# x loaded first, set 0 of the first modulation split in two, and three modulation sets moved into the first loop

## The chip, the cores and the metric

One core of a Trainium2 chip runs the whole block in one launch. The metric is device time in microseconds, the median of three runs.

## What is computed

One layer of a streaming encoder on a sequence of 256 frames of width 2048, in float32. The conditioning vector c gives, through one large matrix, nine vectors of 2048: shift, scale and gate for each of three sublayers.

```python
c_act = silu(c)
mod = c_act @ w_ada + b_ada                      # w_ada 2048 x 18432
sh1, sc1, g1, sh2, sc2, g2, sh3, sc3, g3 = split(mod, 9)
hn = rms(h, norm_ffn1) * (1 + sc1) + sh1
h = h + 0.5 * g1 * (silu(hn @ w1) * (hn @ w3)) @ w2      # first FFN, D_FF 5632
hn = rms(h, norm_mix) * (1 + sc2) + sh2
h = h + g2 * mixer(hn)                           # SSD mixer and sparse attention
hn = rms(h, norm_ffn2) * (1 + sc3) + sh3
h = h + 0.5 * g3 * (silu(hn @ w1b) * (hn @ w3b)) @ w2b   # second FFN
```

## The kernel before

All weights are read once. They come in **units** of 128 x 1024 floats (512 KB), 850 in all. A unit's way: SP loads it into one of four `raw` slots (`load_unit`, L610); ScalarE (ACT) rounds it into `w_hi` (`cast`, L807); VectorE (DVE) forms `w_lo = raw - w_hi` (`sub`, L1246, called the split); TensorE (PE) does twelve matmuls, hi times hi, lo times hi, hi times lo (`unit`, L1948 to L1950). A load waits for the split three units back, a cast for PE's unit four back; every engine works through its own list in order.

`w_ada` comes in **pieces** of 512 KB as well, 128 rows by 1024 columns. VectorE multiplies a piece by its entry of silu(c) and adds it to `ada_acc` (L1356 for the first 64 pieces, L1263 and L1266 for the others): 16 pieces to 1024 columns of the modulation. The first 64 pieces hold shift and scale of the first FFN. They form four sets (`SET_TILES`), each of four column tiles of x; piece m of a set is row block m. Their ring has eight slots (`ada_raw`, `ada_more`). A few pieces (`ADA_SHARE`) are taken by PE (`share`, L1990) instead of VectorE. When a set's pieces are in, PE sums `ada_acc` over partitions with `ones` (`sum_first`, L2029), VectorE adds the bias (`mod_first`, L1302, L1306), ACT modulates the set's tiles of x (`rows_of_set`, L897, L901), and VectorE forms their low part (`lo`, L1396). A unit of w1 or w3 with index u needs tile pair u of x.

The later columns (`ada_add`) have a ring of four; after 16 pieces VectorE folds `ada_acc` (`fold`, L1281, L1284: four transposes and four reductions into `fold_s`), and PE sums the folds at the end of the FFN (`sum_folds`).

The first FFN has an **early** stage of 112 units in an order written out by hand (`EARLY`), so that PE has work on tile pairs that are ready, and then a loop `Fori` of three bodies of 48 units. In the early stage `SUM_AT` says before which unit PE makes a set's sum, `KEPT`, `KEPT_TO` and `ADDED` how partial products are put aside and added again, `UNIT_LOADS` after which piece SP loads a unit, `UNIT_SPLITS` after which piece VectorE splits it. `turn_act` transposes the hidden block, `y_add` (L1461) adds w2 products to y. Pieces 16 to 63 stand between units 3 and 44. Three more sets (`ADA_PEELED`) stand beside units 45 to 104, one piece after 4 of 5 units, and one set in each loop body, one piece after every second unit. The mixer and the second FFN take the rest.

At the start x is loaded behind two pieces; ACT squares it (`square`), VectorE adds the sums (`sum_squares`, L1335), POOL forms rstd (L727), ACT scales x into y (L854), PE transposes y (`turn_x`), ACT stages it (`stage`, L840).

Of the kernel before, what the change touches and what calls it, by code (L numbers as in the profile page):

```python
# [60 lines left out]
ADA_MIX = ADA_FIRST + ADA_PEELED[0] + TRIPS[0]  # L61
# [51 lines left out]
def build(nc, x, c, positions, w_ada, b_ada, norm_ffn1, ffn1_w1, ffn1_w3, ffn1_w2, norm_mix, w_in,  # L113
# [288 lines left out]
    SET_TILES = ((0, 4), (4, 4), (8, 4), (12, 4))  # L402
    SET_START = (0, 16, 32, 48, 64)
# [10 lines left out]
    EARLY = (some("w3", 1, (0, 1)) + some("w1", 0, (0,)) + some("w1", 2, (0, 1)) + some("w1", 0, (1,))  # L414
             + some("w3", 2, (0, 1)) + some("w3", 0, (0,)) + some("w1", 3, (0, 1)) + some("w3", 0, (1,))
# [23 lines left out]
    UNIT_SPLITS = (16, 17, 18, 19) + tuple(19 + (u - 3) * 8 // 7 for u in range(4, LATE[0] - 2))  # L439
# [134 lines left out]
    def ada_unit_after(where, w):  # L574
# [3 lines left out]
        elif where == "trip":  # L578
            at = [6 + 2 * i for i in range(KT)]
# [25 lines left out]
    def _(sp):  # L605
# [634 lines left out]
    def _(dve):  # L1240
# [165 lines left out]
        def norm_first():  # L1406

            turned = [j for j in range(UPB)]
            for m in range(PIECES):
# [11 lines left out]
                if e and at >= 2 and turned and SET_ORDER[turned[0]] < e:  # L1421
# [58 lines left out]
        def early_step(n):  # L1480
# [17 lines left out]
            ada_peeled(0)  # L1498

        def ffn(f):  # L1500
# [25 lines left out]
            def hidden(n, o, adds, w0=0, ada=None, after_second=False):  # L1526


                for u in range(BLOCK):
                    if n.per:  # L1530
                        sub(n + u)
                        k = ada_unit_after("trip", w0 + u)
                        if ada and k is not None:
                            ada_add(At(ada.n0 * KT + k, KT, ada.trip), k)
# [19 lines left out]
            with dve.Fori(0, TRIPS[f]) as trip:  # L1554
                piece = At(ADA_FIRST + ADA_PEELED[0], 1, trip)
# [378 lines left out]
    def _(pe):  # L1934
# [18 lines left out]
        def sum_folds(i, bank):  # L1953
# [4 lines left out]
            pe.wait_ge(fold_step, 2 * (ADA_COLS // FOLD_COLS) * (last - ADA_FIRST))  # L1958
# [570 lines left out]
```

## Time and profile before

| | |
|---|---|
| median of three runs | 2612.09 us (2611.2 to 2614.87) |
| the profiled execution | 2613.14 us |
| its span in the trace | 2611.4 us |
| PE, DVE, ACT busy | 98%, 71%, 44% |
| mean granted clock of PE | 0.989 |
| DMA | 609.98 MB, mean 234 GB/s |

The span runs from the first to the last instruction; 1.7 us lie around it. PE's busy time counts pipelined matmuls to their modelled ends, so a busy PE isn't PE at its peak; how many units a stretch did tells more.

### The profile page before, as it was taken

To read this page: it belongs to the slowest core of one execution; us is meant where nothing else is said; L and a number is where in the kernel's file an instruction comes from. 1 tells how busy PE (TensorE), PEld (TensorE's weight loads), DVE (VectorE), ACT (ScalarE), POOL (GpSimd) and SP (SyncE) were. 2 spreads that over 40 slices of the span, in tenths; PEclk is the share of its full clock that TensorE was granted. 3 is DMA by queue.
4 is the path that set the end of the run, shared out by engine and by line. 5 is a ranking of instruction groups with operands and counts; after the bars stand their busy time and mean duration, and the time that the engine had idled before them with its cause. 6 is when DMAs were issued, how large, how long until landed. Compare 5 with 4: busy or idle time off the path is not lost.

```text
span 2611.4 us, 34332 instructions
## 1 busy us (share of the span) xinstructions
PE 2546.2 (98%) x12494; PEld 2146.7 (82%) x12494; DVE 1852.6 (71%) x2032; ACT 1151.2 (44%) x1365; POOL 68.4 (3%) x72
## 2 busy tenths in 40 slices
PE   6999999999998999999999999999999999999998
PEld 5877888888887999898788888887788888888886
DVE  5779987676766888876876677776679655555555
ACT  4434444444444555544456444443544444444442
POOL 1000000000002000000000000000300000000000
PEclk9989999999999999999999999999999999999999
DMA  9988978787865777744454687787499666666664
GB/s 333 341 308 305 332 274 288 225 284 223 280 225 193 256 263 266 254 145 130 129 169 129 209 289 255 254 285 240 138 317 334 193 193 188 190 192 189 190 192 145
DMA packets 288177, 609.98 MB, mean 234 GB/s; under 512 B 23426, under 2 KB 24004, under 8 KB 287172
## 3 DMA queue, kind: packets, MB, share of 16 engines
q1 hardware_dynamic: 285840, 600.78, 70.0%
q10 hardware_dynamic: 1700, 4.58, 0.5%
q0 software_dynamic: 528, 3.17, 0.3%
q8 instruction: 68, 1.11, 0.2%
q14 instruction: 41, 0.34, 0.0%
HBM read 604.24 MB, written 4.22 MB: 233 GB/s over the span
## 4 chain that ended last, share of the span: by engine, by line
PE 81%; DVE 10%; DMA 5%; issue 3%; ACT 1%; POOL 0%; SPq 0%; DVEq 0%; ACTq 0%; POOLq 0%
PE psum L1948 23%; PE psum L1950 22%; PE psum L1949 22%; PE psum L2227 3%; PE psum L2228 3%; PE psum L2229 3%; PE psum L2250 2%; DVE w_lo L1246 2%; DMA ada_raw<-in_w_ada 2%; PE psum L1936 2%; DMA ada_more<-in_w_ada 1%; DVE ada_acc L1266 1%; DVE ada_acc L1356 1%; DVE y L1461 1%; DMA gate_ffn<-gate_rows 1%
## 5 line engine op out<-in xcount | busy, mean ns | idle before, releaser
L1246 DVE TENSOR_TENSOR w_lo<-raw,w_hi 128x1024 fp32r<-128x1024 f32 x850 | 1034.0, 1221 | 538.8 <-ACT w_hi L807 537.9
L807 ACT ACTIVATE w_hi<-raw 128x1024 fp32r<-128x1024 f32 x850 | 897.2, 1060 | 1010.7 <-PE psum L1950 881.9
L1948 PE MATMUL psum<-w_hi,xT_hi 128*128 128x512 f32 x1984 | 789.3, 398 | 6.9 <-issue 5.2
L1949 PE MATMUL psum<-w_lo,xT_hi 128*128 128x512 f32 x1984 | 777.5, 392 | 0.0
L1950 PE MATMUL psum<-w_hi,xT_lo 128*128 128x512 f32 x1984 | 777.3, 392 | 0.0
L1948 PEld LDWEIGHTS psum<-w_hi,xT_hi 128*128 128x128 f32 x1984 | 375.6, 189 | 89.7 <-issue 11.9
L1950 PEld LDWEIGHTS psum<-w_hi,xT_lo 128*128 128x128 f32 x1984 | 375.2, 189 | 79.3
L1949 PEld LDWEIGHTS psum<-w_lo,xT_hi 128*128 128x128 f32 x1984 | 375.7, 189 | 76.0
L1948 PE MATMUL psum<-w_hi,aT_hi 128*128 128x512 f32 x704 | 277.9, 395 | 7.8 <-DVE aT_lo L1449 4.0
L1950 PE MATMUL psum<-w_hi,aT_lo 128*128 128x512 f32 x704 | 276.3, 392 | 0.0
L1949 PE MATMUL psum<-w_lo,aT_hi 128*128 128x512 f32 x704 | 276.2, 392 | 0.0
L1266 DVE SCALAR_TENSOR_TENSOR ada_acc<-ada_raw,cact,ada_acc 128x1024 f32<-128x1024 f32 x210 | 269.3, 1282 | 0.1
L2227 PE MATMUL psum<-xT_hi,w_hi 128*128 128x256 f32 x640 | 183.6, 287 | 4.9 <-DVE xT_lo L1401 4.3
L2228 PE MATMUL psum<-xT_lo,w_hi 128*128 128x256 f32 x640 | 182.0, 284 | 0.0
L2229 PE MATMUL psum<-xT_hi,w_lo 128*128 128x256 f32 x640 | 182.0, 284 | 0.0
L1948 PEld LDWEIGHTS psum<-w_hi,aT_hi 128*128 128x128 f32 x704 | 133.6, 190 | 37.8 <-DVE aT_lo L1449 4.4
L1950 PEld LDWEIGHTS psum<-w_hi,aT_lo 128*128 128x128 f32 x704 | 133.6, 190 | 28.1
L1949 PEld LDWEIGHTS psum<-w_lo,aT_hi 128*128 128x128 f32 x704 | 133.8, 190 | 27.6
L1461 DVE TENSOR_TENSOR y<-psum,y 128x1024 f32<-128x1024 f32 x101 | 123.3, 1221 | 40.4 <-PE psum L1950 40.4
L2227 PEld LDWEIGHTS psum<-xT_hi,w_hi 128*128 128x128 f32 x640 | 123.3, 193 | 6.0 <-DVE xT_lo L1401 4.9
L2228 PEld LDWEIGHTS psum<-xT_lo,w_hi 128*128 128x128 f32 x640 | 123.5, 193 | 0.0
L2229 PEld LDWEIGHTS psum<-xT_hi,w_lo 128*128 128x128 f32 x640 | 123.4, 193 | 0.0
(252 smaller groups left out, 1937.0 us busy)
## 6 DMA issues: line engine op xcount, KB each, us to landing
raw<-in_ffn_w SPq DMA_DIRECT2D x528, 512.0 KB, 4.5
ada_raw<-in_w_ada SPq DMA_DIRECT2D x256, 512.0 KB, 6.0
raw<-in_w_in SPq DMA_DIRECT2D x224, 512.0 KB, 3.8
ada_more<-in_w_ada SPq DMA_DIRECT2D x32, 512.0 KB, 7.0
raw<-in_w_br_ssd SPq DMA_DIRECT2D x32, 512.0 KB, 5.4
raw<-in_w_br_att SPq DMA_DIRECT2D x32, 512.0 KB, 4.8
raw<-in_w_out SPq DMA_DIRECT2D x32, 512.0 KB, 5.1
h<-in_x SPq DMA_DIRECT2D x1, 2048.0 KB, 9.8
```

Source lines behind the costliest of these rows:

```text
L807: nc.scalar.activation(w_hi[:, n.slot(SPLIT), 0:size], raw[:, n.slot(RAW), 0:size], ACT.Copy).then_inc(hi_ready, 1)
L1246: nc.vector.tensor_tensor(w_lo[:, n.slot(SPLIT), 0:size], raw[:, n.slot(RAW), 0:size], w_hi[:, n.slot(SPLIT), 0:size], ALU.subtract).then_ ...
L1266: nc.vector.scalar_tensor_tensor(out=acc[:], in0=src, scalar=cact[:, k:k + 1], in1=acc[:], op0=ALU.mult, op1=ALU.add).then_inc(ada_used, 1)
L1461: nc.vector.tensor_tensor(y[:, :, cols], psum[:, bank:bank + HALF, :], y[:, :, cols], ALU.add).then_inc(y_added, 1)
L1936: return nc.tensor.transpose(dst, src, ident[0:rows_, 0:rows_])
L1948: nc.tensor.matmul(o, hi[:, kt + k, toks], whi, start=a, stop=False)
L1949: nc.tensor.matmul(o, hi[:, kt + k, toks], wlo, start=False, stop=False)
L1950: ins = nc.tensor.matmul(o, lo[:, kt + k, toks], whi, start=False, stop=b)
L2227: nc.tensor.matmul(o, w_hi[:, s, cols], xT_hi[:, kt + k, :], start=a, stop=False, skip_group_check=True)
L2228: nc.tensor.matmul(o, w_hi[:, s, cols], xT_lo[:, kt + k, :], start=False, stop=False, skip_group_check=True)
L2229: ins = nc.tensor.matmul(o, w_lo[:, s, cols], xT_hi[:, kt + k, :], start=False, stop=b, skip_group_check=True)
L2250: return nc.tensor.matmul(o, a, b, start=first, stop=last)
```

## The change

- SP loads x before any piece.
- The first set of 16 pieces is two of eight: `SET_TILES` has five sets, the first two of two tiles each, and each of their pieces holds two row blocks of 512 columns in two DMAs. The order of the first twelve early units, the points of the sums, loads and splits follow; PE makes the sum of set 0 between the transposes of x, the sum of set 1 before unit 2, of set 2 before unit 13, of sets 3 and 4 before units 26 and 40, as sets 2 and 3 before.
- `ADA_SHARE` keeps its first three pieces; VectorE takes the other three.
- `ADA_PEELED[0]` is 0 and `ADA_TRIP` 2: the early stage has no later pieces, a loop body has 32, three after four units up to unit 42, and two folds. Before, a body had 16, so of the six sets in the loop three are new there.
- The small loads and the exponential of a_exp on ACT stand later; `rows_of_set` follows a cast earlier (n - 2 for n - 3).

```diff
-ADA_SHARE = (1, 6, 11, 30, 46, 62)
+ADA_SHARE = (1, 6, 11)
-ADA_PEELED = (3, 2)
+ADA_PEELED = (0, 2)
+ADA_TRIP = 2
...
-    SET_TILES = ((0, 4), (4, 4), (8, 4), (12, 4))
-    SET_START = (0, 16, 32, 48, 64)
+    SET_TILES = ((0, 2), (2, 2), (4, 4), (8, 4), (12, 4))
+    SET_START = (0, 8, 16, 32, 48, 64)
...
-    EARLY = (some("w3", 1, (0, 1)) + some("w1", 0, (0,)) + some("w1", 2, (0, 1)) + some("w1", 0, (1,))
-             + some("w3", 2, (0, 1)) + some("w3", 0, (0,)) + some("w1", 3, (0, 1)) + some("w3", 0, (1,))
+    EARLY = (some("w1", 0, (0,)) + some("w3", 0, (0,)) + some("w3", 1, (0, 1)) + some("w1", 2, (0, 1))
+             + some("w1", 0, (1,)) + some("w3", 2, (0, 1)) + some("w3", 0, (1,)) + some("w1", 3, (0, 1))
...
-    SUM_AT = {at_unit["w1", 1, 0]: 1, at_unit["w1", 1, 2]: 2, at_unit["w1", 1, 4]: 3}
+    SUM_AT = {at_unit["w3", 1, 0]: 1, at_unit["w1", 1, 1]: 2, at_unit["w1", 1, 2]: 3, at_unit["w1", 1, 4]: 4}
...
-    UNIT_LOADS = (13, 15, 16, 17) + tuple(17 + (u - 3) * 8 // 7 for u in range(4, LATE[0]))
+    UNIT_LOADS = ((3, 5, 8, 11, 14) + tuple(16 + (u - 5) * 4 // 3 for u in range(5, 17))
+                  + tuple(32 + (u - 17) * 8 // 7 for u in range(17, LATE[0])))
...
         elif where == "trip":
-            at = [6 + 2 * i for i in range(KT)]
+            at = [1 + i * 4 // 3 for i in range(ADA_TRIP * KT)]
...
+        sp.dma_start(h[:], x[0].rearrange("(s p) d -> p s d", p=P)).then_inc(x_in, 16)
         for m in range(PIECES):
             load_first(m)
-            if m == 1:
-                sp.dma_start(h[:], x[0].rearrange("(s p) d -> p s d", p=P)).then_inc(x_in, 16)
...
+            cast_units(1)
             act.wait_ge(rstd_ready, 1)
...
-            for j in range(UPB):
+            for j in range(4):
+                stage(0, j)
+            cast_units(2)
+            rows_of_set(0)
+            for j in range(4, UPB):
                 stage(0, j)
             cast_units(SPLIT)
...
-            rows_of_set(0)
-            small_loads()
...
-                if n - 3 in SUM_AT:
-                    rows_of_set(SUM_AT[n - 3])
-                    if SUM_AT[n - 3] == 1:
-                        a_exp_out()
+                if n - 2 in SUM_AT:
+                    rows_of_set(SUM_AT[n - 2])
+                if n == at_unit["w2", 0, 0]:
+                    small_loads()
+                if n == at_unit["w2", 3, 0]:
+                    a_exp_out()
...
+                if m == 2:
+                    sum_squares(0)
...
-                if m == 9:
-                    sum_squares(0)
-                if e and at == 1:
+                if e and at == 0:
                     mod_first(e - 1)
...
-                            ada_add(At(ada.n0 * KT + k, KT, ada.trip), k)
+                            ada_add(At(ada.n0 * KT + k, ada.per * KT, ada.trip), k % KT)
+                            if k % KT == KT - 1:
+                                fold(ada + k // KT)
...
-        share(ADA_SHARE[2])
         warm_up(2)
...
-        sum_first(0)
+            if j == 3:
+                sum_first(0)
         warm_up(3)
+        share(ADA_SHARE[2])
```

PE before its first unit; the y rows are transposes of x, L1990 is a piece taken by PE, L2029 (L2042 after) a sum. Before:

```order
L1990 MATMUL psum<-cact,ada_raw 128x1 x8
L1998 MATMUL psum<-h,ident 128x512 x2
L1936 MATMUL psum<-ident,y 128x128 x32
L2029 MATMUL psum<-ones,ada_acc_103 128x1 x8
L1998 MATMUL psum<-h,ident 128x512 x3
```

After:

```order
L2011 MATMUL psum<-h,ident 128x512 x2
L1946 MATMUL psum<-ident,y 128x128 x16
L2042 MATMUL psum<-ones,ada_acc_103 128x1 x8
L1946 MATMUL psum<-ident,y 128x128 x16
L2011 MATMUL psum<-h,ident 128x512 x3
L2003 MATMUL psum<-cact,ada_raw 128x1 x8
```

The sum of set 0 has moved ahead of half of the transposes, and PE's third piece behind all of them.

VectorE in the loop body, units 5 to 9 (w_lo is a split). Before:

```order
L1246 TENSOR_TENSOR w_lo<-raw,w_hi 128x1024
L1244 REGISTER_ALU
L1246 TENSOR_TENSOR w_lo<-raw,w_hi 128x1024
L1258 ISA
L1263 TENSOR_SCALAR ada_acc_103<-ada_raw,cact 128x1024
L1244 REGISTER_ALU
L1246 TENSOR_TENSOR w_lo<-raw,w_hi 128x1024
L1449 TENSOR_TENSOR aT_lo<-psum,aT_hi 128x1024
L1244 REGISTER_ALU
L1246 TENSOR_TENSOR w_lo<-raw,w_hi 128x1024
L1265 ISA
L1266 SCALAR_TENSOR_TENSOR ada_acc_103<-ada_raw,cact,ada_acc_103 128x1024
```

After:

```order
L1257 TENSOR_TENSOR w_lo<-raw,w_hi 128x1024
L1269 ISA
L1276 REGISTER_ALU
L1277 SCALAR_TENSOR_TENSOR ada_acc_103<-ada_raw,cact,ada_acc_103 128x1024
L1255 REGISTER_ALU
L1257 TENSOR_TENSOR w_lo<-raw,w_hi 128x1024
L1276 REGISTER_ALU
L1277 SCALAR_TENSOR_TENSOR ada_acc_103<-ada_raw,cact,ada_acc_103 128x1024
L1460 TENSOR_TENSOR aT_lo<-psum,aT_hi 128x1024
L1255 REGISTER_ALU
L1257 TENSOR_TENSOR w_lo<-raw,w_hi 128x1024
```

Three of four splits now have a piece behind them.

## Rows read from the trace of the kernel before

**Rows 1.** the page, part 1: busy us, share of the span, instructions.

```profile
PE 2546.2 (98%) x12494; PEld 2146.7 (82%) x12494; DVE 1852.6 (71%) x2032; ACT 1151.2 (44%) x1365; POOL 68.4 (3%) x72
```

**Rows 2.** chain of waits from 46 to 190 us: start us, us, what.

```profile
80.08 6.30 DMA ada_raw<-in_w_ada
```

**Rows 3.** stages, the L1950 matmuls alone, four per unit of weights.

```profile
46.78:86.53 39.75, 19.22 (x48) 9.45 (x48) 0.94 0.97 344
...
182.55:389.90 207.35, 113.65 (x288) 55.01 (x288) 0.98 0.86 302
389.90:786.90 397.00, 224.30 (x576) 108.17 (x576) 1.00 0.76 251
```

**Rows 4.** timeline of VectorE in the loop body, a fold and splits: start us, us.

```profile
640.50 0.44 DVE L1281 STREAM_TRANSPOSE fold_tmp<-ada_acc 128x256 f32<-128x256 f32 x1
...
644.57 2.35 DVE L1246 TENSOR_TENSOR w_lo<-raw,w_hi 128x1024 fp32r<-128x1024 f32 x2
647.52 1.23 DVE L1246 TENSOR_TENSOR w_lo<-raw,w_hi 128x1024 fp32r<-128x1024 f32 x1 [0.60 <-ACT w_hi L807]
650.24 1.23 DVE L1246 TENSOR_TENSOR w_lo<-raw,w_hi 128x1024 fp32r<-128x1024 f32 x1 [1.49 <-ACT w_hi L807]
```

**Rows 5.** timeline of PE around the sum before unit 12.

```profile
81.13 1.84 PE L1990 MATMUL psum<-cact,ada_more 128*128 128x1 f32 x16
84.05 2.62 PE L2029 MATMUL psum<-ones,ada_acc 128*128 128x1 f32 x16 [1.07 <-DVE ada_acc L1356]
...
87.10 0.63 PE L1949 MATMUL psum<-w_lo,xT_hi 128*128 128x512 f32 x1
```

**Rows 6.** stages of 10 us: busy us of each engine, granted clock, DMA share, GB/s.

```profile
20.00:30.00 10.00, 6.78 (x29) 6.22 (x29) 8.26 (x10) 3.19 (x2) 1.99 (x2) 1.00 1.05 387
...
90.00:100.00 10.00, 10.00 (x41) 8.14 (x40) 4.28 (x5) 7.61 (x11) 0.00 (x0) 0.90 0.60 201
```

**Rows 7.** timeline of VectorE at pieces 16, 31, 47 and 63.

```profile
35.00 0.75 DVE L1354 TENSOR_SCALAR ada_acc<-ada_raw,cact 128x1024 f32<-128x1024 f32 x1 [1.39 <-DMA ada_raw<-in_w_ada]
...
82.71 1.28 DVE L1356 SCALAR_TENSOR_TENSOR ada_acc<-ada_more,cact,ada_acc 128x1024 f32<-128x1024 f32 x1 [1.93 <-DMA ada_more<-in_w_ada]
...
130.11 1.28 DVE L1356 SCALAR_TENSOR_TENSOR ada_acc<-ada_more,cact,ada_acc 128x1024 f32<-128x1024 f32 x1 [1.85 <-DMA ada_more<-in_w_ada]
...
178.52 1.28 DVE L1356 SCALAR_TENSOR_TENSOR ada_acc<-ada_more,cact,ada_acc 128x1024 f32<-128x1024 f32 x1 [0.88 <-issue]
```

**Rows 8.** timeline of the SP queue behind piece 31.

```profile
88.73 0.47 SPq L630 DMA_DIRECT2D ada_more<-in_w_ada  x1
96.97 0.37 SPq L610 DMA_DIRECT2D raw<-in_ffn_w  x1
```

**Rows 9.** timeline of PE, unit 0.

```profile
46.78 0.47 PE L1948 MATMUL psum<-w_hi,xT_hi 128*128 128x512 f32 x1 [4.11 <-issue]
```

**Rows 10.** timeline of ACT from the landing of x to the rows of set 0.

```profile
11.59 0.63 ACT L831 ACTIVATE y<-h 128x512 f32<-128x512 f32 x1 [7.04 <-DMA h<-in_x]
...
26.82 3.90 ACT L854 ACTIVATE y<-h,rstd 128x2048 f32<-128x2048 f32 x2 [10.21 <-POOL rstd L727]
...
42.65 1.09 ACT L897 ACTIVATE norm_tmp<-xT_raw,modT,scale_col 128x256 f32<-128x256 f32 x2
...
44.31 1.08 ACT L897 ACTIVATE norm_tmp<-xT_raw,modT,scale_col 128x256 f32<-128x256 f32 x2
```

**Rows 11.** stages: the late early stage, and 132 us of the loop.

```profile
256.00:389.90 133.90, 133.57 (x588) 109.73 (x587) 123.13 (x123) 53.83 (x52) 0.00 (x0) 0.99 0.87 307
400.00:532.00 132.00, 132.00 (x592) 109.54 (x591) 93.10 (x85) 54.62 (x52) 0.00 (x0) 1.00 0.78 255
```

**Rows 12.** timeline of PE behind the first fold.

```profile
254.46 0.50 PE L1948 MATMUL psum<-w_hi,aT_hi 128*128 128x512 f32 x1 [2.19 <-DVE y L1461]
```

**Rows 13.** the tile ada_more: its operations, and what VectorE waited for.

```profile
L1356 DVE SCALAR_TENSOR_TENSOR ada_acc<-ada_more,cact,ada_acc x28: 1272/1284/1289, 16.1 to 178.5; 128x1024 f32<-128x1024 f32 x28
...
  DMA ada_more<-in_w_ada: 16.6, 15
```

More of the change, by code:

```diff
@@ L434, in build @@
              (4, at_unit["w3", 3, 7], 2), (5, at_unit["w1", 4, 7], 0)]
-    SUM_AT = {at_unit["w1", 1, 0]: 1, at_unit["w1", 1, 2]: 2, at_unit["w1", 1, 4]: 3}
+    SUM_AT = {at_unit["w3", 1, 0]: 1, at_unit["w1", 1, 1]: 2, at_unit["w1", 1, 2]: 3, at_unit["w1", 1, 4]: 4}
     TURN_AT = [at_unit["w3", 1, 6], at_unit["w1", 2, 6], at_unit["w1", 3, 5], at_unit["w1", 4, 6]]
     TURN_BANK = [0, 6, 4, 4]
-    UNIT_LOADS = (13, 15, 16, 17) + tuple(17 + (u - 3) * 8 // 7 for u in range(4, LATE[0]))
-    UNIT_SPLITS = (16, 17, 18, 19) + tuple(19 + (u - 3) * 8 // 7 for u in range(4, LATE[0] - 2))
+    UNIT_LOADS = ((3, 5, 8, 11, 14) + tuple(16 + (u - 5) * 4 // 3 for u in range(5, 17))
+                  + tuple(32 + (u - 17) * 8 // 7 for u in range(17, LATE[0])))
+    UNIT_SPLITS = ((6, 8, 11, 14, 17) + tuple(19 + (u - 5) * 4 // 3 for u in range(5, 17))
+                   + tuple(35 + (u - 17) * 8 // 7 for u in range(17, LATE[0] - 2)))
     W2_BANKS = (6, 4, 6, 4)
@@ L452, in early_bank @@
             return RESIDENT[w, block]
+        if n <= KEPT_TO[0]:
+            return 6
         if n < at_unit["w1", 0, 6] or (w, block) == KEPT[0]:
@@ L891, in rows_of_set @@
             act.wait_ge(scale_ready, e + 1)
-            for j in (2 * e, 2 * e + 1):
+            for j in [j for j in range(UPB) if SET_ORDER[j] == e]:
                 if j >= 2:
@@ L905, in keep @@
             act.wait_ge(unit_done, KEPT_TO[i] + 1)
-            nc.scalar.activation(kept(i), psum[:, 4:4 + HALF, :], ACT.Copy).then_inc(part_kept, 1)
+            bank = early_bank(KEPT_TO[i])
+            nc.scalar.activation(kept(i), psum[:, bank:bank + HALF, :], ACT.Copy).then_inc(part_kept, 1)
         def silu_kept(o, i):
@@ L1274, in fold @@
             at = e + -BATCHES[i][0]
-            where = fold_s[:, at.n0, :] if e.per == 0 else fold_s[:, bass.ds(at.trip + at.n0, 1), :]
+            where = fold_s[:, at.n0, :] if e.per == 0 else fold_s[:, bass.ds(at.trip * at.per + at.n0, 1), :]
             dve.wait_ge(ada_used, At((e.n0 + 1) * KT, e.per * KT, e.trip).count())
             for c in range(parts):
-                steps = At(2 * ((e.n0 - ADA_FIRST) * parts + c), 2 * e.per * parts, e.trip)
-                if steps.n0:
-                    dve.wait_ge(fold_step, steps.count())
+                steps = At(1 + 2 * ((e.n0 - ADA_FIRST) * parts + c), 2 * e.per * parts, e.trip)
+                dve.wait_ge(fold_step, steps.count())
                 nc.vector.transpose(fold_tmp[:], ada_acc[0][:, c * FOLD_COLS:(c + 1) * FOLD_COLS]).then_inc(fold_step, 1)
@@ L1420, in norm_first @@
                     early_step(UNIT_SPLITS.index(m))
-                if e and at >= 2 and turned and SET_ORDER[turned[0]] < e:
+                if e and at >= 1 and turned and SET_ORDER[turned[0]] < e:
                     lo(0, turned.pop(0))
@@ L1554, in ffn @@
             with dve.Fori(0, TRIPS[f]) as trip:
-                piece = At(ADA_FIRST + ADA_PEELED[0], 1, trip)
+                piece = At(ADA_FIRST + ADA_PEELED[0], ADA_TRIP, trip)
                 for e in range(2):
@@ L1957, in sum_folds @@
             pe.wait_ge(fold_w_ready, P // FOLD + 1)
-            pe.wait_ge(fold_step, 2 * (ADA_COLS // FOLD_COLS) * (last - ADA_FIRST))
+            pe.wait_ge(fold_step, 1 + 2 * (ADA_COLS // FOLD_COLS) * (last - ADA_FIRST))
             for g in range(P // FOLD):
@@ L1981, in share @@
             e = set_of(m)
-            i = m - SET_START[e]
+            count = SET_TILES[e][1]
+            each = 4 // count
+            k = (m - SET_START[e]) * each
             first = m == min(a for a in ADA_SHARE if set_of(a) == e)
@@ L1989, in share @@
             for j in range(8):
-                ins = nc.tensor.matmul(psum[:, 4 + e % 2, j:j + 1], ada_row(slot)[:, j * P:(j + 1) * P], cact[:, i:i + 1],
+                at, r = j % (2 * count), k + j * each // 8
+                ins = nc.tensor.matmul(psum[:, 4 + e % 2, at:at + 1], ada_row(slot)[:, j * P:(j + 1) * P], cact[:, r:r + 1],
                                        start=first and j == 0, stop=False, skip_group_check=True)
@@ L2080, in early @@
                     e = SUM_AT[n]
-                    if e < SETS - 1:
-                        pe.wait_ge(part_kept, (4, 6)[e - 1])
-                    else:
+                    if e == 2:
+                        pe.wait_ge(part_kept, 4)
+                    if e == 3:
+                        pe.wait_ge(part_kept, 6)
+                    if e == 4:
                         pe.wait_ge(part_added, 2)
-                    share(ADA_SHARE[2 + e])
                     sum_first(e)
@@ L2109, in early @@
                     i = KEPT.index((w, block))
-                    if n < KEPT_TO[3] and i:
-                        pe.wait_ge(part_kept, i)
+                    if n == at_unit["w1", 2, 0]:
+                        pe.wait_ge(mod_ready, 2)
+                    if n == at_unit["w3", 2, 0]:
+                        pe.wait_ge(part_kept, 2)
+                    if n == at_unit["w1", 3, 0]:
+                        pe.wait_ge(part_kept, 3)
                     if n == at_unit["w3", 3, 0]:
-                        pe.wait_ge(mod_ready, 2)
+                        pe.wait_ge(mod_ready, 3)
                     if n == at_unit["w1", 4, 0]:
```

27 lines of the change are left out of this document (14 added, 13 removed).

## The prediction

> **What bounds the kernel now.** I read the page first. PE is busy for 98% of the span [rows 1], so time can only be won where PE waits or runs slowly. The chain of waits names the place: between 46 and 180 us it runs again and again through landings of w_ada pieces, nine of them of 4 to 10 us, of which one stands there [rows 2]. The stage table that counts the L1950 matmuls (four in a unit) gives the rest [rows 3]. In the loop body 144 units take 397.0 us. Splits in the loop follow each other at 2.72 us (647.52 and 650.24) [rows 4], so 391.7 us of this are units and 5.3 us are six transposes of the hidden block, 0.9 us each. The 72 units from unit 40 to the end of the early stage take 207.35 us; 195.8 are units and 3.6 four transposes, about 2.7 a first unit at the lower clock (below), and 5.2 us are lost. Units 0 to 11 take 39.75 us where 32.6 would do, and the granted clock of these stages is 0.94 and 0.98 where the loop has 1.00.
>
> The three later modulation sums are where PE stands. PE first takes a piece of w_ada itself (81.13 us, 1.84 us), then the sum takes 2.6 us at 84.05 (2.5 to the start of unit 12 at 86.53), and that unit's matmuls last 0.63 us [rows 5], where the page's mean is 0.39; the granted clock was at the lower of its two levels, 1.2 GHz, after that thin stretch of one-column matmuls. Such a unit takes twice 2.72 us, so 2.7 us more.
>
> What holds the sums is the stream of the SP queue. I count it in 512-KB equivalents (x is four). Before, piece 16 is used at 35.00 us; with x and two weight units ahead of it that is number 23. Full speed is the row 20 to 30 us: 387 GB/s at a DMA share of 1.05 [rows 6], or 0.524 MB in 1.37 us. Pieces 31, 47 and 63 (numbers 52, 82, 112) are used at 82.71, 130.11 and 178.52 us [rows 7]: 47 to 48 us for 29 or 30 equivalents, 1.6 us each. Some 6.3 us per set are lost (47.4 less 30 times 1.37). The row 90 to 100 us shows where: 201 GB/s, share 0.60 [rows 6]. SP's own rows show how: after a piece at 88.73 it issues nothing until 96.97 [rows 8], because unit loads wait for splits, splits for ACT's casts, and ACT was in rows_of_set and the exponential of a_exp.
>
> **The change, part by part.**
>
> *Start.* Unit 0 starts at 46.78 us [rows 9]. It needs set 0: now 8 pieces, not 16. Piece 7 is number 14 (x 4, pieces 8, units 2): 35.0 less 9 times 1.37 is 22.7, plus 1.0 for the half-size transfers (next paragraph), 23.7. VectorE's op takes 1.3, the sum 2.5, the two small ops behind it about 0.3: 27.8 us. ACT's rows of one tile pair take 1.7 (from 42.65 to 44.31, where the next pair starts) [rows 10], the four stagings left about 2.6: 32.1. PE's own piece 11 (number 19) lands at 30.5 and takes 1.8, as the one at 81.13 [rows 5]: unit 0 starts at 32.3, 14.5 us earlier. x doesn't bind. Its squares began at 11.59 and the scaling at 26.82, after 10.21 us of idling for rstd, as sum_squares stood behind piece 9 [rows 10]. Now x is two pieces earlier (8.9 us), sum_squares stands behind piece 2, and with about 2 us for POOL and 3.9 for the scaling, y is there near 21 us.
>
> *Half-size transfers.* A piece of sets 0 and 1 is two DMAs of 256 KB. No row shows one, so I bound it: 0 at best (same bytes); at worst half the rate, 16 times 1.37, 22 us. I take 1.0 us by piece 15, near the low end, as the nearest rows are the 512-KB transfers at full share [rows 6]. The Trainium skill speaks against the change here: DMA: Bandwidth & Descriptors, Bandwidth, asks for transfers of 1 MiB or more to reach 75% of peak. This trace reaches a share of 1.05 with 512 KB, so it doesn't bear the rule out at that size; what 256 KB do, no run shows yet.
>
> *Set 1.* Piece 15 (number 25) lands at 38.7, the sum ends at 42.5. Units 0 and 1 end at 39.6, with 1.9 us of low clock (the 7.1 us that units 0 to 11 lost before, less the piece's 1.8, the sum's 2.5 and a wait of 0.9 or so). Unit 3 needs the second tile pair: 42.5 plus about 0.4 (the small ops), 1.7 (rows) and 0.7 (the low part) is 45.3. Unit 12 ends at 72.5. This fifth sum is an added wait; it is covered, because the next one ends later anyway.
>
> *Sets 2 to 4.* The stream decides. After each sum ACT still does rows before the next cast, but one cast earlier, without the a_exp table load and exponential, and VectorE's mod_first stands one piece earlier. I work the gap out: issues at about 80.7, 83.9 and 88.5 instead of a gap of 8.24 us [rows 8], where 2.9 is normal. I take 2.5 us lost per set, bounded by 0 and by 6.3. Piece 31 is number 53: 38.7 + 28 x 1.37 + 2.5 = 79.6; VectorE 1.3 and sum 2.5 give unit 13 at 83.4. Thirteen units and 2.7 of low clock end at 121.5. Piece 47: 79.6 + 41.1 + 2.5 = 123.2, unit 26 at 127.0. Fourteen units end at 167.8. Piece 63: 166.8, used at 168.1, **unit 40 starts at 170.6 instead of 182.55: 11.9 us**. The three removed TensorE pieces (1.8 us each) and the three VectorE ops in their place are in these times.
>
> *Units 40 to 111.* 48 pieces and three folds leave VectorE. It was busy 123.13 of 133.90 us [rows 11]; a fold before 254.46 made PE wait 2.19 us for y L1461 [rows 12]. With them goes **5.2 us**. The four transposes stay. The weights alone need 1.37 of 2.72 us per unit, so no transfer comes up instead. The moved small_loads and a_exp stand on ACT, busy for 53.83 us of 133.90 [rows 11]: 0. If that cover were gone, it would be one table load and a cast behind it, about 2 us.
>
> *The three loop bodies.* Each gets 16 more pieces and one more fold: 96 pieces in all. VectorE's ops follow each other at 1.18 us (two in 2.35), a fold takes 4.07 (640.50 to 644.57) [rows 4]. Per body: 48 splits + 32 pieces + 12 others are 92 ops, 108.6 us, plus 8.1: 116.7 of 132.3 us. DMA: 80 x 1.37 = 109.6 us. Both fit. SP and VectorE now do three pieces in four units up to unit 42. The nearest row is the early stage, with four pieces in five units, more additions beside them, and PE at its pace except at folds [rows 11]. A fold that meets four y additions can still use up the lead of the splits: bounds 0 and 6 times 3.9 (the 5.2 us above came with three folds, most of it at one); I take **2 us** in all.
>
> Sum: 11.9 + 5.2 - 2 = 15.1. The profiled execution took 2613.1 us for a span of 2611.4; that gives 2598. It lies 1.05 above the median of 2612.09, so on that scale 2597 us.
>
> **Rivals.**
> - *Forecast, 0.62*: 2597, with 2590 to 2604 for the gap per set.
> - *The stream keeps 1.6 us per equivalent, 0.12.* For it: three sets in a row did [rows 7], and the rings and the wait of unit loads for splits three back are the same. Against: ACT's work behind a sum is shorter. Piece 63 at 38.7 + 88 x 1.6 = 179.5, unit 40 at 183.3: 0.8 lost, 5.2 won, 2 lost, so 2610: the change buys an earlier start and doesn't carry it on.
> - *No gaps and no low clock, 0.18.* Piece 63 at 159.3, unit 40 at 163.1; with 2.7 and 5.2 more and nothing lost in the loop 27.4 won: 2585.
> - *VectorE falls behind in the loop, 0.06.* It works in order, so a piece that lands late holds the splits behind it. Slack is 15.6 us per body: from 0.49 us of waiting per piece it costs, from about 0.74 the whole is slower. Pieces in the early stage waited 16.6 us at 28 ops, 0.59 each [rows 13], at a DMA share near 1; the loop would have between 0.87 (109.6 of 132.3 us at 1.05) and 0.97 (80/64 of the 0.78 it has now [rows 11]). At 0.8 us per piece: 3 x (25.6 - 15.6) = 30 lost, 2627.
> - *Half-size transfers at half rate, 0.02.* All sets 21 us later, 9 later than before at unit 40; less 5.2, plus 2: 2618.
> - That the change isn't what it says: three of the "six" sets were in the loop already (one per body); only three move. This is in the sum.
>
> **How the numbers follow.** A measurement can tell about 0.2%, 5.2 us. Forecast and third case are faster: 0.80. The second is the same: 0.12. The last two are slower: 0.08. The range takes in the second and the third case: 2585 to 2610.
>
> **What would show it.** First unit near 32 us; sum starts near 81, 125 and 168; unit 40 near 171; DMA row 90 to 100 us well over 201 GB/s; no VectorE wait of PE in the later early stage, which ends near 373 instead of 389.9; loop bodies of 132 to 133 us with VectorE at 88 to 90%. I am wrong if unit 40 starts after 180 or a body takes over 135 us.

## The result: 20 us slower, and where they went

The changed kernel takes 2632.8 us (median of four runs, 2631.94 to 2633.62), the kernel before 2612.32 us beside it: a ratio of 1.0077, 95% interval 1.0060 to 1.0094. The prediction was 2597 us with a range of 2585 to 2610, so it had the sign wrong. The profiled execution took 2631.94 us for a span of 2630.2; its page has, for [rows 1]:

```profile
PE 2541.6 (97%) x12462; PEld 2139.9 (81%) x12462; DVE 1861.3 (71%) x2051; ACT 1150.5 (44%) x1365; POOL 67.9 (3%) x72
```

I first cut the span at unit ends, which the trace dates by the semaphore that PE raises behind each unit:

| end of unit (us) | 0 | 3 | 12 | 13 | 26 | 40 | 111 | 255 | 263 | 500 |
|---|---|---|---|---|---|---|---|---|---|---|
| before | 51.4 | 59.5 | 92.0 | 94.8 | 139.1 | 187.9 | 389.9 | 786.9 | 819.2 | 1607.2 |
| after | 45.9 | 56.8 | 89.4 | 95.2 | 152.2 | 210.1 | 406.9 | 803.9 | 838.7 | 1626.9 |
| difference | -5.5 | -2.7 | -2.6 | +0.4 | +13.1 | +22.2 | +17.0 | +17.0 | +19.5 | +19.7 |

The start is 5.5 us earlier, 5.2 us are won from unit 40 to 111, the loop bodies cost nothing, and 25 us are lost between units 12 and 40. Unit 12 flatters the change, as the sum that stood before it now stands before unit 13: unit 11, ahead of both, already ends at 86.2 us for 81.3, so the loss begins behind unit 3. The stages say the same: busy time of the L1960 matmuls (L1950 before) in windows that begin with the first matmul of units 0, 13, 26 and 40, and the loop. Columns: window and length, PE busy, weight loads busy, granted clock, DMA share, GB/s.

```profile
42.85:92.23 49.38, 21.28 (x52) 10.47 (x52) 0.93 0.86 301
92.23:146.97 54.74, 20.83 (x52) 10.19 (x52) 0.92 0.86 293
146.97:204.72 57.75, 23.05 (x56) 11.37 (x56) 0.85 0.75 257
204.72:406.90 202.18, 112.95 (x288) 54.62 (x288) 0.99 0.60 195
406.90:803.90 397.00, 224.11 (x576) 108.11 (x576) 1.00 0.87 311
```

The last two answer to the last two of [rows 3]: 202.18 for 207.35, and 397.00 for 397.00 with 311 in place of 251 GB/s. The second and third are the loss: units 13 to 39 take 112.5 us, where before the 28 units 12 to 39 took 96.0 (86.53 to 182.55), and the DMA share falls to 0.75 in a stretch that the DMA stream bounds.

**What stops the stream.** SP's queue while PE is at units 5 to 8 (start us, us):

```profile
60.24 0.47 SPq L636 DMA_DIRECT2D ada_more<-in_w_ada  x1
60.76 0.47 SPq L636 DMA_DIRECT2D ada_raw<-in_w_ada  x1
62.16 0.37 SPq L616 DMA_DIRECT2D raw<-in_ffn_w  x1
62.58 0.64 SPq L636 DMA_DIRECT2D ada_raw<-in_w_ada  x1
69.00 0.37 SPq L616 DMA_DIRECT2D raw<-in_ffn_w  x1
```

and VectorE in the same microseconds:

```profile
62.45 1.28 DVE L1367 SCALAR_TENSOR_TENSOR ada_acc<-ada_more,cact,ada_acc 128x1024 f32<-128x1024 f32 x1 [0.31 <-DMA ada_more<-in_w_ada]
66.55 1.28 DVE L1367 SCALAR_TENSOR_TENSOR ada_acc<-ada_more,cact,ada_acc 128x1024 f32<-128x1024 f32 x1 [2.82 <-DMA ada_more<-in_w_ada]
67.75 1.22 DVE L1257 TENSOR_TENSOR w_lo<-raw,w_hi 128x1024 fp32r<-128x1024 f32 x1
```

SP issues nothing for 6.4 us. Its next load goes out at 69.00, when the split that began at 67.75 is done. That split stands on VectorE behind a piece that SP had issued at 60.24 and that was there at 66.55, 6.3 us later. SP waits for VectorE, and VectorE for SP's own last transfers: the queue runs dry once per round trip. It repeats at 74.07 to 80.64 and 85.72 to 91.51.

The tables of issue points and split points show why. A load waits for `n - 3` splits, so for the split of the unit four back (the text ahead of the prediction says three). The shortened diff there shows where the loads stand, but not the two lines of the splits, which the change moves as well:

```diff
-    UNIT_LOADS = (13, 15, 16, 17) + tuple(17 + (u - 3) * 8 // 7 for u in range(4, LATE[0]))
-    UNIT_SPLITS = (16, 17, 18, 19) + tuple(19 + (u - 3) * 8 // 7 for u in range(4, LATE[0] - 2))
+    UNIT_LOADS = ((3, 5, 8, 11, 14) + tuple(16 + (u - 5) * 4 // 3 for u in range(5, 17))
+                  + tuple(32 + (u - 17) * 8 // 7 for u in range(17, LATE[0])))
+    UNIT_SPLITS = ((6, 8, 11, 14, 17) + tuple(19 + (u - 5) * 4 // 3 for u in range(5, 17))
+                   + tuple(35 + (u - 17) * 8 // 7 for u in range(17, LATE[0] - 2)))
```

Before, a split stands two pieces behind its own load, after it three. Four units are 4 x 8/7 = 4.57 pieces, so the split that a load waits for stood 4.57 - 2 = 2.57 pieces ahead of the newest piece issued; now it is 4 x 4/3 - 3 = 2.33 for units 5 to 16 and 4.57 - 3 = 1.57 from unit 17 on. That is what SP may have in flight beyond the awaited split. This became the theory, **theory L** (lookahead). Its rival, theory R in the expectations, was the order on ACT: rows_of_set now stands one cast earlier, and holds that cast. A third theory was that VectorE now takes three pieces more, which PE took before.

### The profile page after: what moved, and what is told of

It is laid out like the page before. It is cut to its first block, busy times and chain, and to the rows that moved or that the text cites. A ratio compares the mean times of both kernels' runs of the same rounds, so it can differ in the third digit from the quotient of the medians.

```text
span 2630.2 us, 34499 instructions
## 1 busy us (share of the span) xinstructions
PE 2541.6 (97%) x12462; PEld 2139.9 (81%) x12462; DVE 1861.3 (71%) x2051; ACT 1150.5 (44%) x1365; POOL 67.9 (3%) x72
## 4 chain that ended last, share of the span: by engine, by line
PE 87%; DVE 6%; DMA 3%; issue 2%; ACT 1%; SPq 1%; POOL 0%; DVEq 0%; ACTq 0%; POOLq 0%
PE psum L1958 25%; PE psum L1959 24%; PE psum L1960 24%; PE psum L2248 3%; PE psum L2249 3%; PE psum L2250 3%; PE psum L2271 2%; PE psum L1946 2%; DVE w_lo L1257 1%; DMA ada_more<-in_w_ada 1%; DMA gate_ffn<-gate_rows 1%; DVE ada_acc L1367 1%; DVE y L1593 1%; DMA ada_raw<-in_w_ada 0%; PE psum L2042 0%
## 5 line engine op out<-in xcount | busy, mean ns | idle before, releaser
L1960 PE MATMUL psum<-w_hi,xT_lo 128*128 128x512 f32 x1984 | 777.0, 392 | 0.0
L1960 PEld LDWEIGHTS psum<-w_hi,xT_lo 128*128 128x128 f32 x1984 | 375.1, 189 | 79.9
L1960 PE MATMUL psum<-w_hi,aT_lo 128*128 128x512 f32 x704 | 275.2, 391 | 0.0
L1960 PEld LDWEIGHTS psum<-w_hi,aT_lo 128*128 128x128 f32 x704 | 132.9, 189 | 27.9
```

What stands on the lines that cost most here:

```text
L1960: ins = nc.tensor.matmul(o, lo[:, kt + k, toks], whi, start=False, stop=b)
```

## The experiments

Ratios are against the kernel before, run beside each kernel on the same chip (its medians were 2613.3 to 2614.1 us). "Before" in a diff's sentence is the kernel the edit is made in. Ends of units are of one profiled execution each; how far two of them scatter, e12 shows. The profiled execution isn't always near its kernel's median: 2.6 us below it in e2, 2.4 below in e3, 3.2 above in e5.

**e1_loop_only**: the kernel before, with the loop part of the change alone.

```diff
-ADA_PEELED = (3, 2)
+ADA_PEELED = (0, 2)
+ADA_TRIP = 2
...
-            at = [6 + 2 * i for i in range(KT)]
+            at = [1 + i * 4 // 3 for i in range(ADA_TRIP * KT)]
```

> The kernel before with the loop part alone: no later modulation pieces in the early stage, 32 per loop body. Theory A (this part gains what its term said, and the loss lies ahead of unit 40): units 40 to 111 take 196.8 us instead of 202.0 and a body stays at 132.3, so 5 us faster than before, about 2607 us. Theory B (three bodies at 93% of VectorE and the fuller DMA give something back behind the loop, as the 35 us after the last body hint): no gain, 2610 to 2613.

Measured: 2608.6 us, ratio 0.9979 (0.9969 to 0.9988). Unit 40 ends at 188.4, unit 111 at 385.2, 196.8 us later, as in the changed kernel (before: 202.0), and unit 255 at 782.2. So this part is a gain by itself, and the loss lies in the other part.

**e2_rows_after_cast**: in the changed kernel, rows_of_set goes back behind the cast.

```diff
-                if n - 2 in SUM_AT:
-                    rows_of_set(SUM_AT[n - 2])
+                if n - 3 in SUM_AT:
+                    rows_of_set(SUM_AT[n - 3])
```

> The changed kernel, with ACT's rows_of_set again behind the cast of unit sum+3 (n - 3 instead of n - 2). Theory R (the cast that now stands behind the rows holds VectorE's split and with it the SP queue, 2.1 us of VectorE idling at set 2 and 4.4 at set 3): 6 to 12 us faster than the changed kernel, 2621 to 2627. Theory L (what holds the stream is that splits follow their loads three pieces later, so a load waits for a split that stands behind the newest piece): at most 3 us, 2630 to 2633.

Measured: 2630.19 us, ratio 1.0063 (1.0047 to 1.0080), which overlaps the change's. From unit 13 to unit 40 it takes 109.7 us (99.9 to 209.6) where the change takes 114.9, but unit 13 comes 4.7 us later. By the medians 2.6 us hang on this order, by the two ratios 3.7, and neither is told from nothing; it isn't what costs 20 us.

**e3_rows_and_splits**: e2 with the splits of units 5 to 42 one piece earlier, two behind their loads as before.

```diff
-    UNIT_SPLITS = ((6, 8, 11, 14, 17) + tuple(19 + (u - 5) * 4 // 3 for u in range(5, 17))
-                   + tuple(35 + (u - 17) * 8 // 7 for u in range(17, LATE[0] - 2)))
+    UNIT_SPLITS = ((6, 8, 11, 14, 17) + tuple(18 + (u - 5) * 4 // 3 for u in range(5, 17))
+                   + tuple(34 + (u - 17) * 8 // 7 for u in range(17, LATE[0] - 2)))
```

> As the run before, and the splits of units 5 to 42 one piece earlier, so two pieces behind their loads as in the kernel before. Theory L: the gaps of 4 to 7 us in SP's issues go, the 1.9 us per 512 KB of the sets 2 to 4 fall to 1.6 or less: 15 to 20 us off, 2605 to 2615. Theory R: nothing beyond the run before. A third theory (the three pieces that VectorE took over from TensorE, and three more of its operations, hold the stream): neither run helps, both stay over 2625.

Measured: 2611.13 us, ratio 0.9990 (0.9980 to 0.9999). Unit 13 to unit 40 takes 95.1 us (94.1 to 189.2). One number in two formulas brings back 19 us, nearly the size of the change's net loss.

**e4_late_splits_in_before**: the same from the other side, the kernel before with its splits one piece later.

```diff
-    UNIT_SPLITS = (16, 17, 18, 19) + tuple(19 + (u - 3) * 8 // 7 for u in range(4, LATE[0] - 2))
+    UNIT_SPLITS = (16, 17, 18, 19) + tuple(20 + (u - 3) * 8 // 7 for u in range(4, LATE[0] - 3))
```

> The kernel before with its splits from unit 4 on one piece later, nothing else. Theory L: the lead of the loads shrinks as in the changed kernel, so 10 to 20 us slower than before, 2622 to 2632. Theory R and the third theory: no change, 2612, as VectorE has the same work in nearly the same order.

Measured: 2632.67 us, ratio 1.0074 (1.0057 to 1.0091), unit 40 at 206.8 for 187.9. Everything else is as before, so the splits' place alone makes a loss as large as the change's, and VectorE's three added pieces aren't needed for it. The tile ada_more, half of the pieces' ring, shows it in one line, what VectorE (and once PE) waited for its landings, us and times. Before it was 16.6 us in 15 [rows 13]. The changed kernel:

```profile
  DMA ada_more<-in_w_ada: 33.6, 23
```

e3:

```profile
  DMA ada_more<-in_w_ada: 15.5, 15
```

e4:

```profile
  DMA ada_more<-in_w_ada: 40.2, 22
```

The transfers themselves were not slower: the median from issue to landing of this tile is 6.4 us in the changed kernel and 6.8 in e3. They were issued late. The other half of the ring, ada_raw, differs little up to 215 us: 23.9 us before, 24.9, 20.3 and 26.2 in these three.

**e5_splits_two_earlier**: e3 with the splits of units 4 to 29 another piece earlier.

```diff
-    UNIT_SPLITS = ((6, 8, 11, 14, 17) + tuple(18 + (u - 5) * 4 // 3 for u in range(5, 17))
-                   + tuple(34 + (u - 17) * 8 // 7 for u in range(17, LATE[0] - 2)))
+    UNIT_SPLITS = ((6, 8, 11, 14, 16) + tuple(17 + (u - 5) * 4 // 3 for u in range(5, 17))
+                   + tuple((33 if u < 30 else 34) + (u - 17) * 8 // 7 for u in range(17, LATE[0] - 2)))
```

> As e3_rows_and_splits, with the splits of units 4 to 42 another piece earlier (one piece behind their loads). Theory L with room left: the stream still loses 0.1 to 0.2 us per 512 KB in e3, so 5 to 8 us off, 2603 to 2606. Rival (now VectorE waits for the cast of a unit whose load has only just been issued, and its own pieces stand behind that wait): the lead of the loads is no longer what binds and the time is that of e3 or up to 10 us more, 2611 to 2621.

The edit moves units 4 to 29; the expectation says 4 to 42.

Measured: 2608.17 us, ratio 0.9981 (0.9971 to 0.9991), unit 40 at 191.5. The second piece brings 3 us by the medians, with overlapping intervals, and none at unit 40 in this one profiled execution. The first piece brought 20 there (209.6 to 189.2).

**e6_start_on_vector**: e3 with piece 6 on VectorE, so that PE's warm-up stands ahead of the landing it would wait for.

```diff
-ADA_SHARE = (1, 6, 11)
+ADA_SHARE = (1, 11)
...
-        share(ADA_SHARE[1])
         warm_up(2)
...
-        share(ADA_SHARE[2])
+        share(ADA_SHARE[1])
```

> As e3_rows_and_splits, with piece 6 on VectorE instead of TensorE, so that TensorE's warm-up matmuls and the transposes of x do not stand behind the landing of that piece. Theory: y was scaled at 21.8 us and the transposes began at 29.9 only; they now begin near 22, the sum of set 0 ends near 27 instead of 34.8, and unit 0 starts 6 to 8 us earlier. If the earlier start is carried through the sets, the whole takes 2604 to 2606; if the stream alone decides (rival), unit 0 starts earlier and unit 40 doesn't, 2610 to 2612.

The rows behind it, PE at the start of the changed kernel:

```profile
22.97 3.54 PE L2003 MATMUL psum<-cact,ada_more 128*128 128x1 f32 x16 [6.24 <-DMA ada_more<-in_w_ada]
26.38 3.76 PE L2011 MATMUL psum<-h,ident 128*128 128x512 f32 x4
29.93 3.26 PE L1946 MATMUL psum<-ident,y 128*128 128x128 f32 x16
33.02 1.84 PE L2042 MATMUL psum<-ones,ada_acc 128*128 128x1 f32 x16
```

y was there at 21.8 us and VectorE's last addition to set 0 ended near 25.8, but PE waited for piece 6, multiplied it, ran its warm-up matmuls and half of the transposes, and made the sum at 33.02. VectorE stood behind that sum, with splits and pieces queued behind the bias:

```profile
34.90 0.16 DVE L1312 TENSOR_TENSOR modT<-psum,badaT 128x4 f32<-128x4 f32 x1 [8.16 <-PE psum L2042]
```

Measured: 2606.62 us, ratio 0.9971 (0.9961 to 0.9982). The sum of set 0 starts at 26.7, unit 0 ends at 41.6 (e3: 45.5), unit 40 at 185.6 (e3: 189.2). Behind the sum 11.8 us pass to unit 0 (38.55), as the other transposes, more warm-up matmuls and piece 11 stand there. By the ratios the earlier start is worth 5.0 us against e3, and 3.7 with e12, the same kernel once more: it is carried to the end, but the intervals of e12 and e3 overlap.

**e7_tensor_pieces_back**: e3 with pieces 30, 46 and 62 on PE again, ahead of the sums.

```diff
-ADA_SHARE = (1, 6, 11)
+ADA_SHARE = (1, 6, 11, 30, 46, 62)
...
+                    if e >= 2:
+                        share(ADA_SHARE[1 + e])
```

> As e3_rows_and_splits, with pieces 30, 46 and 62 on TensorE again, ahead of the sums of the last three sets. If leaving them out was worth its term: 3 x 1.84 us slower, 2616 to 2617. Rival (TensorE waits there anyway, and VectorE has one piece less in the stream's way): no difference, 2610 to 2612.

Measured: 2613.44 us, ratio 0.9997 (0.9987 to 1.0006), unit 40 at 192.7. Against e3 it is 2.3 us, between the two forecasts, and the intervals overlap.

**e8_before_loop_and_splits**: e1 (the loop part in the kernel before) with every early split one piece earlier and mod_first behind a set's first piece.

```diff
-    UNIT_SPLITS = (16, 17, 18, 19) + tuple(19 + (u - 3) * 8 // 7 for u in range(4, LATE[0] - 2))
+    UNIT_SPLITS = (15, 16, 17, 18) + tuple(18 + (u - 3) * 8 // 7 for u in range(4, LATE[0] - 2))
...
-                if e and at == 1:
+                if e and at == 0:
```

> The kernel before (sets of 16 pieces, x behind two pieces) with the loop part, its splits one piece earlier and mod_first one piece earlier. Theory L with room left: 3 x 3 us off against the loop part alone, 2598 to 2602. Rival (at two pieces the lead is enough and the gaps behind a sum remain): 2606 to 2609.

Measured: 2609.55 us, ratio 0.9983 (0.9974 to 0.9993). Not told apart from e1 (0.9979). Unit 0 comes later (55.0 for 52.2), unit 13 too (102.5 for 93.0), and unit 40 is where it was (187.8 for 188.4). An earlier split is not free. VectorE stands 6.53 us for the cast of the first split, with piece 16 behind it, which is used at 41.37 us where e1 used it at 34.91:

```profile
40.22 1.23 DVE L1247 TENSOR_TENSOR w_lo<-raw,w_hi 128x1024 fp32r<-128x1024 f32 x1 [6.53 <-ACT w_hi L808]
```

**e9_free_pieces**: e6 with the splits of units 17 to 23 and 31 to 37 one piece later, and that of unit 30 two. The expectation says more (17 to 24 one, 30 to 38 two); the formula gives this.

```diff
-                   + tuple(34 + (u - 17) * 8 // 7 for u in range(17, LATE[0] - 2)))
+                   + tuple(max(34 + (u - 17) * 8 // 7, u + 18 if u < 25 else u + 20 if 30 <= u < 39 else 0)
+                           for u in range(17, LATE[0] - 2)))
```

> The kernel of e6 (span 2603.4 us, unit 40 at 185.6 us), with the splits of units 17 to 24 one piece later and those of units 30 to 38 two pieces later, so that behind the sums of sets 2 and 3 no VectorE split is due of a unit that needs a product made after the sum. Theory G (what is left at a sum is VectorE standing in order behind a cast that waits for the first unit after the sum: w_lo 5.13 us behind w_hi in e6, an SP gap of 8.9 us there): the gaps at sums 2 and 3 shrink by 3 to 4 us each, unit 40 ends 5 to 7 us earlier, near 180 us, and the time is 2599 to 2602 us. Rival L (a later split shortens the lookahead of the stream, as one piece did in e4 for +18.6 us, and this outweighs the freer sums): unit 40 at 187 to 195 us, time 2608 to 2615 us.

What it aims at are VectorE's rows behind the sum of set 3 in e6. The split waits for a cast, the cast for PE's first unit after the sum, and the pieces of the next set stand behind it:

```profile
131.28 0.17 DVE L1312 TENSOR_TENSOR modT<-psum,badaT 128x8 f32<-128x8 f32 x1 [1.88 <-PE psum L2042]
131.48 0.16 DVE L1316 SCALAR_TENSOR_TENSOR scale_col<-modT,vecT 128x4 f32<-128x4 f32 x1
136.77 1.23 DVE L1257 TENSOR_TENSOR w_lo<-raw,w_hi 128x1024 fp32r<-128x1024 f32 x1 [5.13 <-ACT w_hi L812]
```

Measured: 2613.14 us, ratio 0.9998 (0.9989 to 1.0008), unit 40 at 194.9. Theory G fell, rival L held. VectorE does flow now, in e9:

```profile
136.21 1.28 DVE L1367 SCALAR_TENSOR_TENSOR ada_acc<-ada_raw,cact,ada_acc 128x1024 f32<-128x1024 f32 x1
138.11 0.69 DVE L1407 TENSOR_TENSOR xT_lo<-norm_tmp,xT_hi 128x512 fp32r<-128x512 f32 x1 [0.62 <-ACT xT_hi L911]
138.72 1.28 DVE L1367 SCALAR_TENSOR_TENSOR ada_acc<-ada_raw,cact,ada_acc 128x1024 f32<-128x1024 f32 x1
141.42 1.23 DVE L1257 TENSOR_TENSOR w_lo<-raw,w_hi 128x1024 fp32r<-128x1024 f32 x1 [1.42 <-ACT w_hi L812]
```

but SP does not, since its next load awaits that same split, wherever it stands:

```profile
133.81 0.47 SPq L636 DMA_DIRECT2D ada_raw<-in_w_ada  x1
142.67 0.37 SPq L616 DMA_DIRECT2D raw<-in_ffn_w  x1
```

An SP gap of 8.9 us, as long as the one in e6 (129.17 to 138.02). So the later split costs lookahead and opens no gap. That this cost falls in the rest of the set is argued from the table, not measured apart.

**e10_x_behind_two**: e6 with x loaded behind two pieces again.

```diff
-        sp.dma_start(h[:], x[0].rearrange("(s p) d -> p s d", p=P)).then_inc(x_in, 16)
         for m in range(PIECES):
             load_first(m)
+            if m == 1:
+                sp.dma_start(h[:], x[0].rearrange("(s p) d -> p s d", p=P)).then_inc(x_in, 16)
```

> The kernel of e6 with x loaded behind two pieces of w_ada again, as in the kernel before, all else as in e6 (unit 0 at 41.6 us, median 2606.6 us). Theory X (x first is worth what its load is earlier, since the squares, y and the transposes hang on it): unit 0 ends 2 to 6 us later and the time is 2609 to 2612 us. Rival N (the sums of the first set are what the first unit waits for, and they want the pieces, not x): unit 0 within 1 us of e6 and the time 2605 to 2608 us.

Measured: 2608.45 us, ratio 0.9978 (0.9968 to 0.9987), unit 0 at 45.0. Unit 0 is 3.4 us later than in e6 but 1.7 later than in e12, and e12's ratio is 0.9976. The time lies between the two theories' ranges. What x first brings is not told apart from nothing.

**e12_start_again** and **e11_start_and_two_earlier**: e6 once more, and e6 with e5's splits.

> The kernel of e6 once more, in five rounds, beside e11 on one chip. If e6 is faster than the kernel before, the ratio is again 0.996 to 0.998 with an upper end below 1, and unit 40 ends within 3 us of 185.6 us.

> The kernel of e6 with the splits of units 4 to 16, of units 17 to 29 one piece earlier again. Theory L in its simple form (every piece by which the awaited split stands further ahead of the newest piece gives time) wants unit 40 5 us or more ahead of e12 and the time near 2600 us. Theory L with saturation (once the issues of SP aren't bound by the splits, only the sums' own stops are left, as e5 gained only 3 us over e3 in time and none at unit 40): within 3 us of e12, 2604 to 2608 us.

Measured: e12 2606.54 us, ratio 0.9976 (0.9967 to 0.9985), unit 40 at 187.8; e6 had 185.6, so an end of a unit scatters by 2 us. e11 2602.68 us, ratio 0.9964 (0.9950 to 0.9977), unit 40 at 183.6: the best kernel of the study, faster than before by 0.36%. Against e12 it is 3.9 us by the medians and 4.2 at unit 40, between what the two forms of theory L expected. The intervals of the two ratios overlap, but the kernels ran side by side on one chip, and four of e11's five executions (2601.83 to 2603.61 us) lie below all eleven of e12 (2604.09 to 2607.91). So a second piece of lookahead does bring 3 to 4 us. The wait for landings of ada_more is 8.5 us in 15 waits in e12, and has nearly gone in e11:

```profile
  DMA ada_more<-in_w_ada: 4.2, 6
```

That of ada_raw is still 16.7 us (20.4 in e12, both up to 215 us). The stops at the sums are left too, as behind the sum of set 3:

```profile
134.84 1.22 DVE L1257 TENSOR_TENSOR w_lo<-raw,w_hi 128x1024 fp32r<-128x1024 f32 x1 [5.17 <-ACT w_hi L812]
```

## Why the prediction was wrong, step by step

- **The step that failed: "2.5 us lost per set"** in *Sets 2 to 4*, and under it the sentence in the second rival that "the rings and the wait of unit loads for splits three back are the same". The wait is the same; the place of what it waits for is not. I had worked the gap from the one stop behind the sum [rows 8] and taken the stream at full speed everywhere else. Pieces 31 and 63 (60 equivalents apart) were used at 89.07 and 199.93 us, 1.85 us each, not (41.1 + 2.5) / 30 = 1.45; that is 0.4 x 60 = 24 us, and 14.3 us lost per set. Moving the splits alone makes 19 (e3) and 18.6 us (e4, by the medians; 20.1 by the spans, 2631.5 less 2611.4).
- **With the splits left where they were, the 2.5 would still have been too small.** In e3, with the splits two pieces behind their loads, the same pieces are used at 84.44 and 179.08 us: 1.58 us each, the pace of the kernel before, and 6.2 us lost per set. Even e11 keeps 1.53 (81.41 to 173.37 us), 4.9 per set. The 2.5 came from shorter work on ACT behind a sum; with a_exp's exponential out of the way there (e3 has rows_of_set behind its cast again) no run shows the pace that it promised. Of the 36 us between forecast and measurement the splits are 19 (e3 against e2), e2's order 2.6 that isn't told from nothing, and e3 is still 14 above the forecast. This pace and the start below are what the traces show in those 14; they aren't separated further.
- **Start, 32.3 us; measured 42.85.** The data came as forecast (y at 21.8 for "near 21", set 0 complete at 25.8 for 25.0). I had set PE's own queue ahead of the sum at nothing: piece 6, the warm-up and 16 transposes stood there, and the sum began at 33.02 in place of 25. Behind it PE took 9.8 us to unit 0 where I had 7.3. A TensorE piece was priced at 1.8 us from the one at 81.13; at the start it takes 3.54, and the kernel before already showed that:

```profile
25.62 3.54 PE L1990 MATMUL psum<-cact,ada_raw 128*128 128x1 f32 x16 [3.22 <-DMA ada_raw<-in_w_ada]
```

  e6 gets 6.3 us of it back at the sum, 3.9 at unit 0, and 4.5 in the time (3.7 by e12's ratio).
- **Half-size transfers, +1.0 us.** The stretch at full share with them in it moved

```profile
20.00:30.00 10.00, 7.03 (x21) 4.89 (x22) 5.42 (x10) 1.83 (x1) 0.00 (x0) 1.00 1.09 355
```

  355 GB/s for 387 at 1.05 [rows 6], 8% less, so by those two rows 16 x 1.37 x 0.09 = 2 us by piece 15. Right in kind, half in size; half rate is excluded. The Trainium skill, DMA: Bandwidth & Descriptors, Bandwidth, asks for transfers of 1 MiB or more to reach 75% of the peak. The prediction held a DMA share of 1.05 against that, but a share is the time that the engines were busy, not a part of the peak. What can be held against it are the rates: 387 GB/s with 512 KB, and 355 with 256-KB transfers among them. No run shows the peak, so the rule itself isn't tested here; by these two rows the smaller transfers cost about 8%, with 512-KB unit loads among them in the second.
- **"One cast earlier" as a help**: no run shows a gain from it. e2 takes it back and is 2.6 us faster by the medians, which isn't told from nothing.
- **TensorE's pieces at 1.84 us each**: 5.5 us in the forecast, 2.3 by e7, and not told from nothing. PE waits for the last piece of the set anyway; that this hides the rest is argued.
- **Units 40 to 111, 5.2 us**: right, 207.35 less 202.18 in the trace and again in e1.
- **Loop, 2 us lost; measured 0.** VectorE was forecast at 116.7 of 132.3 us:

```profile
400.00:532.00 132.00, 132.00 (x593) 109.45 (x591) 114.47 (x108) 53.59 (x51) 0.00 (x0) 1.00 0.86 303
```

  114.47 of 132, share 0.86 for 0.78 [rows 11], and 397.00 us for the three bodies. The rival by which VectorE falls behind there is out.
- **Not forecast**: 2.5 us between units 255 and 263. VectorE waits for the gate rows,

```profile
820.60 1.23 DVE L1593 SCALAR_TENSOR_TENSOR y<-gate_ffn,y 128x1024 f32<-128x1024 f32 x1 [4.87 <-DMA gate_ffn<-gate_rows]
```

  where the kernel before waits 0.88. e2 and e3 have the same loop part, and this stretch takes 32.7 and 32.5 us there, against 34.8 in the change and 32.3 before. So it isn't bound to the change's loop part; why this execution had it stays open.

The rival "the stream keeps 1.6 us per equivalent" had the right mechanism with too small a price. Its price was the old pace; nothing in it let the pace get worse than before. Where the splits stand as before, in e3, it comes out: unit 40 starts at 183.88 us for its 183.3, and the time is 2611.13 for its 2610. For the change itself the gap in the cases was this: the rival that would have been right is "the splits' new place shortens what SP has in flight", to be read from two lines of the diff against SP's rows. The criterion named for being wrong, unit 40 after 180, did fire (its first matmul is at 204.72). Two of the prediction's numbers don't follow from its own rows: the landings of 4 to 10 us in the chain between 46 and 180 us are ten, not nine, and in the VectorE rival the whole is slower from about 0.65 us of waiting per piece, not 0.74 (15.1 us won over three bodies is 5.0 each; with the slack of 15.6 that is 20.6 over 32 pieces).

## What to carry to other kernels

Where one in-order queue issues loads that wait for a consumer, and that consumer stands in order behind other loads of the same queue, what counts is how many issues lie between the awaited operation and the newest load. Work it out for before and after from the tables of positions. Here one position less (2.57 to 1.57) cost 19 to 20 us, and one more than before gained only 3 to 4, so the price isn't the same per position. A transfer that waits for nothing on the DMA side can still be late: look at who its issuing queue waited for. And of an earlier start, cost the engine's own queue ahead of the operation, not only the arrival of its data.

## What the runs showed of the hardware

The granted clock is low around the longest stalls, and that makes them dearer. These are the stretch from 196 to 210 us of the changed kernel, with PE idle for 7.77 us ahead of the last sum, and that of the sum before unit 13:

```profile
196.00:210.00 14.00, 8.68 (x29) 7.61 (x30) 6.58 (x9) 4.29 (x7) 0.00 (x0) 0.51 0.45 149
90.45:92.37 1.92, 1.92 (x17) 1.92 (x18) 1.70 (x2) 0.00 (x0) 0.00 (x0) 1.00 0.78 298
```

In the first the clock is at its lower level, 1.2 GHz (0.51), in the second at the higher. The sum's 16 one-column matmuls take 3.54 us at the lower one and 1.92 at the higher:

```profile
90.45 1.92 PE L2042 MATMUL psum<-ones,ada_acc 128*128 128x1 f32 x16 [1.07 <-issue]
...
201.32 3.54 PE L2042 MATMUL psum<-ones,ada_acc 128*128 128x1 f32 x16 [7.77 <-issue]
```

The first came after 1.07 us of idling, the second after 7.77.

One trap lies in this column. PE's pieces at 12.15 and 22.97 us of the changed kernel also took 3.55 and 3.54 us, although the row from 20 to 30 us gives 1.00. The trace's first record of the clock begins at 32.4 us; ahead of it the column shows 1.00 for want of a record, and the lengths of the matmuls speak for the lower level.
